# GpSimd instead of VectorE makes the rests of the second layer's output weights

## The reference

```python
for l in range(DEPTH):                       # DEPTH = 2
    hn = rmsnorm(x, norm_g[l])
    proj = hn @ w_in[l]                      # 1024 -> 3072
    u, g_main, q_mem, g_mem = jnp.split(proj, ...)
    if l < N_A:                              # layer 0: convolution and linear recurrence
        ...
    else:                                    # layer 1: sliding-window attention, window 128, with sinks
        q = rope(u.reshape(B, T, N_HEADS, HEAD_DIM), pos)
        ...
        y = sink_attend(q, k_att, v_att, mask, sinks[l - N_A]).reshape(B, T, D_MAIN)
    om = mem_attend(q_mem, mem_k[l], mem_v[l])
    z = jnp.concatenate([y * silu(g_main), om * silu(g_mem)], axis=-1)   # 1536 columns
    x = x + z @ w_out[l]                     # 1536 -> 1024
return rmsnorm(x, final_g), ...
```

## Time and profile before

| | |
|---|---|
| median of three runs | 2064.64 us |
| the profiled execution | 2065.78 us |
| its span | 2064.0 us |
| PE busy | 2048.7 us (99%) |
| DVE busy | 1175.9 us (57%) |
| ACT busy | 922.9 us (45%) |
| POOL busy | 121.9 us (6%) |

### The profile page before, as it was taken

One profiled execution on the slowest core, in us unless ns is written; L12 is line 12 of the kernel. 1 busy time (PEld: TensorE's weight loads), 2 busy tenths in 40 slices (PEclk: granted clock), 3 DMA queues, 4 the chain that ended last, 5 costly groups with the idle time before them and its releaser, 6 DMA issues.

```text
span 2064.0 us, 34681 instructions
## 1 busy us (share of the span) xinstructions
PE 2048.7 (99%) x14497; PEld 1626.3 (79%) x14497; DVE 1175.9 (57%) x2029; ACT 922.9 (45%) x2015; POOL 121.9 (6%) x138
## 2 busy tenths in 40 slices
PE   9999999999999999999999999999999999999998
PEld 7888887777777777777888888777778778777886
DVE  4845436777777842222634444688888888833232
ACT  5733335777777832222533433444444445422111
POOL 0000000000000000000200000222121220000000
PEclk9999999999999999999999999999999999999999
DMA  9311111111110565354211111222222214485352
GB/s 384 144 64 41 64 39 52 48 59 49 45 47 29 189 218 183 121 168 138 93 54 36 39 44 39 60 77 80 70 86 68 78 58 142 136 274 173 114 187 94
DMA packets 118828, 210.66 MB, mean 102 GB/s; under 512 B 12596, under 2 KB 67924, under 8 KB 114184
## 3 DMA queue, kind: packets, MB, share of 16 engines
q1 hardware_dynamic: 118672, 208.45, 30.0%
HBM read 160.00 MB, written 48.48 MB: 101 GB/s over the span
## 4 chain that ended last, share of the span: by engine, by line
PE 92%; DVE 5%; ACT 1%; DMA 1%; issue 1%; SPq 0%; DVEq 0%
PE bank L611 51%; PE bank L2094 23%; PE bank L153 2%; PE bank L715 2%; PE bank L1175 2%; PE bank L451 2%; PE bank L1161 2%; PE bank L702 2%; PE bank L911 1%; DVE wo_lo L1788 1%; PE bank L631 1%; PE bank L705 1%; DVE in_x L351 1%; DMA z_raw<-z_scratch 1%; DMA mk_w<-in_w_mem_kv 0%
## 5 line engine op out<-in xcount | busy, mean ns | idle before, releaser
L611 PE MATMUL bank<-x_hi,w_hi 128*128 128x512 f32 x1600 | 636.6, 398 | 0.4 <-DVE w_lo L597 0.4
L611 PE MATMUL bank<-x_hi,w_lo 128*128 128x512 f32 x1600 | 624.5, 390 | 0.0
L611 PE MATMUL bank<-x_lo,w_hi 128*128 128x512 f32 x1600 | 623.6, 390 | 0.0
L611 PEld LDWEIGHTS bank<-x_hi,w_hi 128*128 128x128 f32 x1600 | 300.4, 188 | 96.5 <-issue 35.4
L611 PEld LDWEIGHTS bank<-x_hi,w_lo 128*128 128x128 f32 x1600 | 300.4, 188 | 64.3
L611 PEld LDWEIGHTS bank<-x_lo,w_hi 128*128 128x128 f32 x1600 | 300.8, 188 | 60.6 <-issue 0.7
L2094 PE MATMUL bank<-wo_hi,z_hi 128*128 128x512 f32 x768 | 304.5, 396 | 4.3 <-DVE z_lo L1817 3.7
L2094 PE MATMUL bank<-wo_lo,z_hi 128*128 128x512 f32 x768 | 299.6, 390 | 0.0
L2094 PE MATMUL bank<-wo_hi,z_lo 128*128 128x512 f32 x768 | 299.4, 390 | 0.0
L2094 PEld LDWEIGHTS bank<-wo_hi,z_hi 128*128 128x128 f32 x768 | 144.2, 188 | 43.5 <-issue 5.0
L2094 PEld LDWEIGHTS bank<-wo_hi,z_lo 128*128 128x128 f32 x768 | 144.2, 188 | 30.5
(11 more groups left out here) (324 smaller groups left out, 2625.4 us busy)
## 6 DMA issues: line engine op xcount, KB each, us to landing
w_raw<-in_w_items SPq DMA_DIRECT2D x25, 1024.0 KB, 5.1
z_scratch<-it_gz SPq DMA_DIRECT2D x96, 256.0 KB, 2.6
z_raw<-z_scratch SPq DMA_DIRECT2D x32, 768.0 KB, 5.6
it_cs<-in_rope SPq DMA_DIRECT2D x32, 512.0 KB, 4.2
wo_raw<-in_w_out SPq DMA_DIRECT2D x6, 2048.0 KB, 9.9
in_rows<-in_x_prompt SPq DMA_DIRECT2D x4, 2048.0 KB, 26.4
in_x<-in_x_T SPq DMA_DIRECT2D x4, 2048.0 KB, 26.8
z_x<-in_x_prompt SPq DMA_DIRECT2D x16, 512.0 KB, 5.0
```

Source lines behind the costliest of these rows:

```text
L611: last = nc.tensor.matmul(ps, s_, r_, start=(k == 0 and q == 0), stop=(k == KT - 1 and q == 2))
```

## The change

The twelve instructions that make `wo_lo` of the second layer are taken from DVE and given to POOL. DVE loses `behind_dve` altogether and the `weights_low` calls in `within_dve`; it still makes `z_lo` in iterations 31 and 32. POOL makes the twelve slices in order, k = 0 to 11, each after its `wo_hi[k]`, between its last input weights and its two memsets. The first layer is as before. No wait of PE, ACT or SP is changed.

```diff
@@ swa_dve
             if q < NQ:
                 gate_product(v, "main", *ipc(q))
-            ahead["behind_dve"](v, q)
@@ output
+    def weights_low_pool(g):
+        for k in range(NI):
+            g.wait_ge(whi, nw + k + 1)
+            nc.gpsimd.tensor_tensor(m.wo_lo[:, k, :], m.wo_raw[:, k, :], m.wo_hi[:, k, :].bitcast(F32), ALU.subtract).then_inc(wlo, 1)
+
     def within_dve(v, q):
-        if q == 30:
-            weights_low(v, 0, range(0, 2))
         if q in (31, 32):
             split_dve(v, q - 31)
-        if q == 32:
-            weights_low(v, 2, range(0, 2))
-
-    def behind_dve(v, q):
-        if q == 30:
-            weights_low(v, 0, range(2, 4))
-        if q == 31:
-            weights_low(v, 1)
-        if q == 32:
-            weights_low(v, 2, range(2, 4))
@@ the program of POOL
                 it1["swa_pool"](g)
+                op1["weights_low_pool"](g)
                 sm1["pool"](g)
```

More of the change, by code:

```diff
@@ L1881, in within_dve @@
     def within_dve(v, q):
-        if q == 30:
-            weights_low(v, 0, range(0, 2))
         if q in (31, 32):
             split_dve(v, q - 31)
-        if q == 32:
-            weights_low(v, 2, range(0, 2))
-    def behind_dve(v, q):
-        if q == 30:
-            weights_low(v, 0, range(2, 4))
-        if q == 31:
-            weights_low(v, 1)
-        if q == 32:
-            weights_low(v, 2, range(2, 4))
-    ahead = dict(early_sp=early_sp, late_sp=late_sp, within_act=within_act, behind_act=behind_act, within_dve=within_dve, behind_dve=behind_dve, weights_sp=ahead_weights_sp, tiles_sp=ahead_tiles_sp, rows_sp=ahead_rows_sp, weights_act=ahead_weights_act,
+    ahead = dict(early_sp=early_sp, late_sp=late_sp, within_act=within_act, behind_act=behind_act, within_dve=within_dve, weights_sp=ahead_weights_sp, tiles_sp=ahead_tiles_sp, rows_sp=ahead_rows_sp, weights_act=ahead_weights_act,
                  tiles_act=ahead_tiles_act, dve=ahead_dve, first_dve=ahead_first_dve)
@@ L2194, in output @@
     made = dict(w_ld=w_ld, z_ld=z_ld, x_ld=x_ld, signals=signals, ahead=ahead, sync=sync, stored=stored,
-                scalar=scalar, vector=vector, tensor=tensor, half=half, first=first, mmd=mmd, xn=xn, yn=yn, sx=sx)
+                scalar=scalar, vector=vector, tensor=tensor, half=half, first=first, weights_low_pool=weights_low_pool, mmd=mmd, xn=xn, yn=yn, sx=sx)
     if l == 0:
```

## The result

The kernel after the change takes 2071.22 us (median of 8 runs, 2070.21 to 2073.13), the kernel before beside it 2065.01 us (8 runs, 2064.3 to 2066.35). The ratio is 1.003, with a 95% interval from 1.0021 to 1.0039: slower, by 6.2 us, and above 2068.8, from which on the prediction counts a kernel as slower. The forecast was 2069.0, which lies 2.2 us under it.

The account below looks back on a forecast made before the run. PE was taken to bound the kernel, with 5.0 us of waits behind DVE. POOL turns cost +7.4 us, reduced to +4.4 by slices and `z_lo` 1 in time; 2064.64 + 4.4 gave 2069.0 us, range 2065.2 to 2073.4.

Parts of the forecast that it names:

- the second rival: Item 29 is hit like item 30: PE's turning at 1754.8 is 5.2 us late, +8.1 in all, 2072.7; chance 0.20.
- Step 1: POOL's first four rests, from 1738.2: L669 waits hidden, L1282 ends 2.1 us late, removed L1788 pays; PE sees nothing.
- Step 2: Next four rests: L1282 waits 1.9 us, `z_lo` 0 starts late, PE's first L2094 at 1766.3 not 1764.76: +1.6 us.
- Step 3: Near 1770, L1301, L1290, L1292 wait 1.7, 2.2, 1.95 behind POOL; PE turns P at 1778.35: +7.4 us in all.
- Step 4: Slices 4 to 7 are there without waits, giving back 1.3 us: +6.1 at the values of item 30.
- Step 5: `z_lo` 1 runs 1786.35 to 1788.0; PE goes on at 1788.15 not 1783.05: +5.1, its wait 0.9 not 1.74.
- Step 6: Twelve slices without a wait give back 0.7 us: +4.4 us at 1796.4, from there all as before.
- the small operations pass: L1282 and L1290, reading 8 elements, slip past POOL; only L1301 and L1292 wait in step 3: +1.0 us, 2065.6; chance 0.11.
- there is no mutual exclusion: POOL and DVE don't obstruct each other here; PE's 5.0 us of waits go: 2059.6 us, faster; chance 0.07.

Follow-up runs that it names:

- e3: Changed kernel, but POOL makes only the first eight rests and DVE the last four at their old places: 2063.43 us.
- e1: Changed kernel with nobody making the second layer's rests; PE multiplies by `wo_hi` again in their place: 2059.45 us.
- e5: Kernel without second-layer rests, plus eight DVE operations of 128x512 that change nothing, ahead of item 30's normalisation; POOL makes no rests: 2066.93 us.
- e4: Changed kernel with POOL's twelve subtractions replaced by memsets, same waits and signals; PE multiplies by `wo_hi` in place of the rest: 2059.79 us.
- e7: Changed kernel, all twelve rests on POOL, but the last four start only when item 30's normalisation is done: 2065.72 us.
- e2: Changed kernel with POOL making each rest in four pieces of 128x256, order unchanged: 2064.35 us.
- e8: POOL makes the first eight rests, the eighth cut in four pieces, DVE the last four: 2062.63 us.
- e6: Kernel without second-layer rests, plus four DVE operations of 128x512 that change nothing, ahead of item 30's normalisation: 2062.83 us.

## Why the prediction came out as it did

The mechanism, the sign and the places were right, and the size fell 1.8 us short (+4.4 against 6.2). That the sign came out is not worth much by itself: the forecast of 2069.0 lay 0.2 us above the mark of 2068.8, and the prediction gave "slower" 0.49. The time is inside the range of 2065.2 to 2073.4, but 0.4 above the narrower one that the prediction gave its own course, 2067.5 to 2070.8; the room above that had been left for the second rival, and it is nearer to that rival's 2072.7 than to the forecast. This is luck: the rival's course was not taken, as shown below. Step by step, with the 0.6 us that after is late ahead of the stage taken off:

- **Step 1** (hidden): L669 at 1738.85 takes 2.89 and L1282 2.07; L1292 starts at 1753.95 (1753.3 + 0.6) and PE sees nothing. Right.
- **Step 2** (+1.6): L1282 takes 2.07, PE's first L2086 is at 1766.28 for 1764.76, +1.5. Right.
- **Step 3** (+7.4): the three turns cost L1301 2.1, L1290 2.2 and L1292 1.9; PE turns at 1778.59 for 1770.97, +7.6. Right (5.9 were forecast for the three together, 6.1 measured), and e3, which takes only P8 to P11 away from POOL, shows that it is these. PE's wait there was forecast at 6.6 us and is 5.14, since PE ran the slices ahead of it at the low clock of 0.57 and came to the turning 1.4 us later; that cost nothing here.
- **Step 4** (gives back 1.3, +6.1 at the values): the values are at 1788.11 for 1779.74, +8.4. This is the step that failed, as its sum has eight slices, the turning and the scores at the durations of before. The slices were there in time; but turning, scores and the first slice ran at a clock of 0.50. From the turning to the values after takes 9.52 us, e1 at full clock 7.56: 2.0 us that had no term. e5 shows that the long wait alone brings this.
- **Step 5** (+5.1, with a wait of 0.9 for `z_lo` 1): DVE had `z_lo` 1 at 1788.24 and so on the predicted 1788.0 nearly, but PE came only at 1789.6, +6.55. By estimate: at full clock PE would have been there at 1787.64 (1789.6 - 1.96) and gone on behind `z_lo` at about 1788.4, so of the 2.0 us some 0.8 took the place of the wait that was predicted, and 1.2 came on top.
- **Step 6** (gives back 0.7): 0.5 given back, +6.04 at the last L153. PE has no wait for `wo_lo` of layer 1, as said.

So the sum lacks one term, TensorE's clock behind the long wait, worth by this estimate 1.2 us of the 1.6 by which the stage was mis-sized; 0.2 are `z_lo` 1 being ready later and 0.2 step 6. The forecast's argument stopped at when PE may go on, and did not ask how fast it would then go.

**The rivals.** That the small operations pass is refuted: L1282 and L1290 take 2.07 and 2.32. That item 29 is hit like item 30 did not occur: L1292 took 1.23 at 1753.95, and PE turned at 1755.42, that is 1754.82 for the 1754.8 of before. It started at 1753.95 and P4 asked at 1754.05, so that turn was decided by 0.1 us. That there is no mutual exclusion is refuted for subtractions on POOL, and e4 shows a condition under which it would have been right: POOL only writes. The 2059.6 us given for that case are what e1 and e4 measure, 2059.45 and 2059.79.

**What stays open.** The Trainium skill's section cited in the prediction says that the loser blocks fully, and this case agrees, row by row, where POOL's instruction has two inputs. What decides the turns when both ask at nearly the same time was read from the order of starts, not tried by itself. Nor was a POOL instruction of this length with one input.

## What to carry to other kernels

Work moved from DVE to an idle POOL is not free if POOL's instructions have two SBUF inputs while DVE has such instructions too: each of DVE's then stands for up to one whole POOL instruction, be it 8 columns wide or 1024. So look at the short DVE instructions that gate other engines, and either place POOL's work where DVE reads PSUM or one input (e7), move only the part that meets nothing (e3), or cut it into shorter instructions just where it meets something (e2, e8). And price a new long wait of TensorE above its own length: here 5.1 us of waiting cost 7.1 to 7.5 up to the next product with the values.

## What was not expected of the hardware

A wait of PE of 5.1 us brings the granted clock to 0.50 (1.2 GHz) for about 4 us behind it, in after and in e5 alike, and costs 2.0 and 2.4 us. Behind shorter waits it is not uniform: behind 2.34 us in after it was 0.57 between 1766 and 1770 (matmuls 0.43 us apart and not 0.228), and behind 2.32 in e7 0.59 in the same window, but behind 2.32 in e3, ahead of the same instruction, 1.00:

```profile
1766.00:1770.00 4.00, 3.82 (x17) 1.00 1.13 347
```

```profile
1766.00:1770.00 4.00, 3.86 (x10) 0.59 1.05 348
```

(the first of e3, the second of e7; 17 against 10 matmuls in the same 4 us). In e6, behind 2.16 us, it stayed at 1.00 as well. In e7 the turning came 1.04 us after that of e3 (1773.43 for 1772.39), though L1292 had started within 0.04 us of the other (1771.07 and 1771.11): that is the price of the lower clock there, taken up later by the wait for `z_lo` 1. In after PE waited for P anyway. What decides in a single execution is open.
